# Attention probabilities left unnormalised in a two-block float32 transformer kernel: row sums from the value product, scaling behind it

## What is computed

```python
# GQA: 8 query heads, 2 key/value heads, width 64; MLA: 8 heads, width 96 (keys) and 64 (values)
def blocked_attention(q, k, v, scale):
    ...
    def one_block(qblk):                      # 128 queries
        sc = jnp.einsum('bqhgd,bkhd->bhgqk', qblk, k).astype(jnp.float32) * scale
        p = jax.nn.softmax(sc, axis=-1).astype(v.dtype)
        return jnp.einsum('bhgqk,bkhd->bqhgd', p, v)

# token mixer: ya = GQA attention, yb = MLA attention
merged = g_a * (ya @ w_branch_a) + g_b * (yb @ w_branch_b)
return merged @ w_o
```

## Time and profile before

| | us |
|---|---|
| three runs: median (lowest to highest) | 2943.45 (2938.77 to 2945.5) |
| the profiled execution's own time | 2941.37 |
| its span, first to last instruction | 2939.6 |
| TensorE busy with matmuls | 2820.3 (96%) |
| VectorE, ScalarE, GpSimd busy | 1624.9, 1168.5, 753.2 |

### The profile page before, as it was taken

One profiled execution on the slowest core, in us unless ns is written; L12 is line 12 of the kernel. 1 busy time (PEld: TensorE's weight loads), 2 busy tenths in 40 slices (PEclk: granted clock), 3 DMA queues, 4 the chain that ended last, 5 costly groups with the idle time before them and its releaser, 6 DMA issues.

```text
span 2939.6 us, 34972 instructions
## 1 busy us (share of the span) xinstructions
PE 2820.3 (96%) x13382; PEld 2333.7 (79%) x13382; DVE 1624.9 (55%) x2135; ACT 1168.5 (40%) x1840; POOL 753.2 (26%) x625
## 2 busy tenths in 40 slices
PE   8998999999988999999999888999999999999998
PEld 6676888888876768878888776888887789888887
DVE  5787446334267864464542896555533458565532
ACT  5575334222255753342222554332322338532322
POOL 2464113313125631133131271022200003122210
PEclk9999999999999999999999999999999989999999
DMA  3011222323220112223232211222232210123233
GB/s 138 29 44 37 96 98 80 101 94 100 93 79 29 44 37 95 99 79 108 93 101 93 91 26 61 96 98 96 98 108 93 84 53 1 58 94 97 96 100 101
DMA packets 76279, 236.50 MB, mean 80 GB/s; under 512 B 9904, under 2 KB 19904, under 8 KB 76128
## 3 DMA queue, kind: packets, MB, share of 16 engines
q1 hardware_dynamic: 74928, 231.05, 24.0%
q0 software_dynamic: 928, 3.27, 0.3%
q10 hardware_dynamic: 272, 0.06, 0.0%
HBM read 228.31 MB, written 2.10 MB: 78 GB/s over the span
## 4 chain that ended last, share of the span: by engine, by line
PE 85%; DVE 7%; ACT 3%; issue 2%; SPq 1%; POOL 1%; DMA 1%; POOLq 0%; DVEq 0%; ACTq 0%
PE bank L2063 27%; PE bank L2065 26%; PE bank L2064 26%; PE bank L2472 2%; PE bank L2297 2%; SPq L949 1%; DVE X L1623 1%; DMA RAWW<-weights 1%; DVE STAT L1724 1%; DVE WL L1594 1%; DVE UL L1611 1%; DVE FF L1618 1%; ACT WH L1234 1%; PE bank L2240 0%; DVE FF L1638 0%
## 5 line engine op out<-in xcount | busy, mean ns | idle before, releaser
L1594 DVE TENSOR_TENSOR WL<-RAWW,WH 128x1024 fp32r<-128x1024 f32 (+2 forms) x424 | 573.0, 1355 | 745.2 <-ACT WH L1234 745.0
L2063 PE MATMUL bank<-UH,WH 128*128 128x512 f32 (+2 forms) x1968 | 768.8, 391 | 32.8 <-DVE UL L1611 11.5
L2064 PE MATMUL bank<-UL,WH 128*128 128x512 f32 (+2 forms) x1968 | 760.2, 386 | 0.0
L2065 PE MATMUL bank<-UH,WL 128*128 128x512 f32 (+2 forms) x1968 | 760.2, 386 | 0.0
L1234 ACT ACTIVATE WH<-RAWW 128x1024 fp32r<-128x1024 f32 (+2 forms) x424 | 431.3, 1027 | 401.9 <-DMA RAWW<-weights 401.3
L2063 PEld LDWEIGHTS bank<-UH,WH 128*128 128x128 f32 (+1 forms) x1968 | 372.1, 189 | 119.7 <-issue 22.9
L2064 PEld LDWEIGHTS bank<-UL,WH 128*128 128x128 f32 (+1 forms) x1968 | 372.2, 189 | 75.6 <-issue 2.4
L2065 PEld LDWEIGHTS bank<-UH,WL 128*128 128x128 f32 (+1 forms) x1968 | 371.8, 189 | 75.1
L2063 PE MATMUL bank<-HH,WH 128*128 128x512 f32 (+1 forms) x576 | 210.8, 366 | 0.0
L2065 PE MATMUL bank<-HH,WL 128*128 128x512 f32 (+1 forms) x576 | 210.5, 365 | 0.0
L2064 PE MATMUL bank<-HL,WH 128*128 128x512 f32 (+1 forms) x576 | 210.5, 365 | 0.0
(11 more groups left out here) (366 smaller groups left out, 4783.3 us busy)
## 6 DMA issues: line engine op xcount, KB each, us to landing
RAWW<-weights SPq DMA_DIRECT2D x424, 512.0 KB, 3.4
X<-x SPq DMA_DIRECT2D x8, 256.0 KB, 5.0
FF<-tables POOLq DMA_DIRECT2D x2, 1024.0 KB, 7.9
U<-S5U SPq DMA_DIRECT2D x32, 64.0 KB, 2.0
out<-FF SPq DMA_DIRECT2D x16, 128.0 KB, 1.8
GEL<-U SPq DMA_DIRECT2D x112, 16.0 KB, 1.8
S5B<-s_b POOLq DMA_DIRECT2D x1, 512.0 KB, 4.5
S5C<-s_c POOLq DMA_DIRECT2D x1, 512.0 KB, 3.7
```

What stands on the lines that cost most here:

```text
L1594: dve.tensor_tensor(slot_words(WL, c % SLOTS, size), slot_words(RAWW, c % SLOTS, size), f32(slot_words(WH, c % SLOTS, size)), ALU.subtract ...
L2063: nc.tensor.matmul(out_, w[0], x_[0], start=start, stop=False, **how)
L2064: nc.tensor.matmul(out_, w[0], x_[1], start=False, stop=False, **how)
L2065: return nc.tensor.matmul(out_, w[1], x_[0], start=False, stop=stop, **how)
```

## The change

Seven edits go together.

1. The exponential has no accumulated sum any more, VectorE no reciprocal, GpSimd no multiplication. The tile that is transposed is the exponential itself. `TMP` has three buffers for it and not four; the fourth becomes `Y`.
2. The stationary high part of the values has 64 columns of ones beside the head's 64 value columns (`values_high`), so bank 6 holds the head's unnormalised output on rows 0 to 63 and the row sums, repeated, on rows 64 to 127. The low part has 64 columns alone. The number of matmuls is the same.
3. Behind the values ScalarE takes the logarithm of the sums from the bank and then exp(-log) in place (`att_out_sum`), VectorE multiplies the output by that into `Y` (`att_out_scale`, which frees bank 6), ScalarE copies the high part (`att_out_cut`) and VectorE subtracts (`att_out_low`).
4. Every stage from the transpose on moves one `x` earlier against the scores: transpose at `u + 2`, `att_lo` at `u + 3`, the values from `4h + 7`, `att_out_sum` and `att_out_scale` at `4h + 10`, `att_out_cut` and `att_out_low` at `4h + 11`.
5. GpSimd writes ones (a memset of 128 x 512 at the start of a layer, two of 128 x 256 before the MLA values) in place of zeros (four of 128 x 256).
6. `VL` is made by two VectorE instructions of half the size.
7. To make room, two constant matrices are loaded later with the mask, and the second block's parameters (`SP_`) are loaded by GpSimd's queue in the second layer and not at the very start.

```diff
     for x in range(n + 8):
-        h, phase = divmod(x - KT - 4, KT)
+        h, phase = divmod(x - KT - 3, KT)
+        if 1 <= h <= 2 * HEADS and phase == 0:
+            plan.add("att_out_cut", h=h - 1, pv=h - 1)
         if 0 <= h < 2 * HEADS and phase == 3:
-            plan.add("att_out_hi", h=h, pv=h)
+            plan.add("att_out_sum", h=h, pv=h)
...
-        if 1 <= x <= n:
-            plan.add("att_normalise", u=x - 1)
-        if 3 <= x <= n + 2:
-            plan.add("att_transpose", u=x - 3, h=(x - 3) // KT, t=(x - 3) % KT)
+        if 2 <= x <= n + 1:
+            plan.add("att_transpose", u=x - 2, h=(x - 2) // KT, t=(x - 2) % KT)
...
+        if 1 <= h <= 2 * HEADS and phase == 0:
+            plan.add("att_out_low", h=h - 1, pv=h - 1)
+        if 3 <= x <= n + 2:
+            plan.add("att_lo", u=x - 3, h=(x - 3) // KT, t=(x - 3) % KT)
         if 0 <= h < 2 * HEADS and phase == 3:
-            plan.add("att_out_lo", h=h, pv=h)
+            plan.add("att_out_scale", h=h, pv=h)
...
+        Y = TMP[:, RING, :]
+        def values_high(h, k):
+            if h < HEADS:
+                return VH[:, k, h % 2 * 2:h % 2 * 2 + 2, :].rearrange("p g d -> p (g d)")
+            return MVH[:, h % 2, k, :]
...
-                elif st.kind == "att_normalise":
-                    pool.wait_ge(recip.sem, recip.after(l, st.u))
-                    pool.tensor_tensor(TMP[:, st.u % 4, :], TMP[:, st.u % 4, :],
-                                       STAT[:, 2, st.u % 4:st.u % 4 + 1].to_broadcast([P, SEQ]), ALU.mult
-                                       ).then_inc(normed.sem, 1)
...
-                    act.activation(TMP[:, r, :], BANK[2 + st.u % 2][:], ACT.Exp, bias=STAT[:, 0, r:r + 1],
-                                   accum_out=STAT[:, 1, r:r + 1]).then_inc(expd.sem, 1)
+                    act.activation(TMP[:, st.u % RING, :], BANK[2 + st.u % 2][:], ACT.Exp, bias=STAT[:, 0, r:r + 1]
+                                   ).then_inc(expd.sem, 1)
...
+                elif kind == "att_out_sum":
+                    act.wait_ge(pv.sem, pv.after(l, st.pv))
+                    if st.h:
+                        act.wait_ge(y_l.sem, y_l.after(l, st.pv - 1))
+                    act.activation(Y[0:HD, :], OUTB[HD:P, :], ACT.Ln).then_inc(y_log.sem, 1)
+                    act.wait_ge(y_log.sem, y_log.after(l, st.pv))
+                    act.activation(Y[0:HD, :], Y[0:HD, :], ACT.Exp, scale=-1.0).then_inc(y_factor.sem, 1)
+                elif kind == "att_out_cut":
                     h, _, rows, k = pv_place(st.h)
-                    act.wait_ge(pv.sem, pv.after(l, st.pv))
-                    act.activation(h[rows, k, :], OUTB[rows, :], ACT.Copy).then_inc(y_h.sem, 1)
+                    act.wait_ge(y_scaled.sem, y_scaled.after(l, st.pv))
+                    act.activation(h[rows, k, :], Y[rows, :], ACT.Copy).then_inc(y_h.sem, 1)
...
-                elif kind == "att_normalise":
-                    r = st.u % 4
-                    dve.wait_ge(expd.sem, expd.after(l, st.u))
-                    dve.reciprocal(STAT[:, 2, r:r + 1], STAT[:, 1, r:r + 1]).then_inc(recip.sem, 1)
...
-                elif kind == "att_out_lo":
+                elif kind == "att_out_scale":
+                    _, _, rows, _ = pv_place(st.h)
+                    dve.wait_ge(y_factor.sem, y_factor.after(l, st.pv))
+                    dve.tensor_tensor(Y[rows, :], OUTB[0:HD, :], Y[0:HD, :], ALU.mult).then_inc(y_scaled.sem, 1)
+                elif kind == "att_out_low":
                     h, lo_, rows, k = pv_place(st.h)
                     dve.wait_ge(y_h.sem, y_h.after(l, st.pv))
-                    rest(lo_[rows, k, :], OUTB[rows, :], h[rows, k, :]).then_inc(y_l.sem, 1)
+                    rest(lo_[rows, k, :], Y[rows, :], h[rows, k, :]).then_inc(y_l.sem, 1)
...
                         if st.h:
-                            pe.wait_ge(y_l.sem, y_l.after(l, st.h - 1))
+                            pe.wait_ge(y_scaled.sem, y_scaled.after(l, st.h - 1))
...
                     for k in st.keys:
-                        v = (VH[:, k, :], VL[:, k, :]) if st.h < HEADS else (MVH[:, st.h % 2, k, :], MVL[:, st.h % 2, k, :])
-                        ins = product(OUTB[:], v, (ph[:, k, :], pl[:, k, :]), k == 0, k == KT - 1)
+                        nc.tensor.matmul(OUTB[:], values_high(st.h, k), ph[:, k, :], start=k == 0, stop=False)
+                        nc.tensor.matmul(OUTB[0:HD, :], values_low(st.h, k), ph[:, k, :], start=False, stop=False)
+                        ins = nc.tensor.matmul(OUTB[:], values_high(st.h, k), pl[:, k, :], start=False, stop=k == KT - 1)
```

More of the change, by code:

```diff
@@ L80 @@
 LAST_BANK, FACTOR_BANK = 2, 7
+RING = 3
 LAST_LEAD, POST_MIX, POST_FFN = 2, 4 + QT, 7 + QT
@@ L700, in build @@
         SPARE = at("SPARE", A0 + 16, [P, 2, SEQ])
-        VH = at("VH", A0 + 20, [P, KT, P], F32R)
-        VL = at("VL", A0 + 22, [P, KT, P], F32R)
+        VH = at("VH", A0 + 20, [P, KT, 4, HD], F32R)
+        VL = [at(f"VL{k}", kb, [P, KT // 2, P], F32R) for k, kb in enumerate((204.5, 206))]
         CH = at("CH", A0 + 24, [P, CQT + CKT, SEQ], F32R)
@@ L776, in build @@
         PA = at("PA", 207, [P, 5, PAIRS])
-        MASK = at("MASK", 98, [P, P])
+        MASK = at("MASK", 98, [P, 3, P])
         IDENT, ONES, ONES_HEAD = (MAT[:, k, :] for k in range(3))
-        ROT_A, ROT_B, NEG_TRI, NEG_ONES = (MATR[:, k, :] for k in range(4))
+        ROT_A, ROT_B = (MATR[:, k, :] for k in range(2))
+        NEG_TRI, NEG_ONES = (NEG[:, k, :] for k in range(2))
         BANK = [ctx.enter_context(nc.psum_tensor(f"bank{k}", [P, SEQ], F32)) for k in range(8)]
@@ L806, in build @@
         mats_cut = ctx.enter_context(nc.semaphore("mats_cut"))
-        mv_zero, k_zero = (ctx.enter_context(nc.semaphore(k)) for k in ("mv_zero", "k_zero"))
+        v_ones, mv_ones, k_zero, sp_params = (ctx.enter_context(nc.semaphore(k)) for k in ("v_ones", "mv_ones", "k_zero", "sp_params"))
         x_done = signal("x_done", "x", PN)
@@ L869, in own_square, with pv_place @@
             return {"q": (None, RKV[:], RCQ[:], spare[0]), "cq": (spare[1], RKV[:], RCQ[:]), "ckv": (spare[1], RKV[:])}[st.what][st.i]
+        def pv_place(h):
+            if h < HEADS:
+                a = h % 2 * HD
+                return QH, QL, slice(a, a + HD), h // 2
+            m = h - HEADS
+            return YBH, YBL, slice(m % 2 * HD, m % 2 * HD + HD), m // 2
         def raw(st):
@@ L1020, in step @@
                     pool.tensor_tensor(CL[:, k, :], CF[:, k, :], f32(CH[:, k, :]), ALU.subtract).then_inc(c_l.sem, 1)
[L1021 to L1025 removed]
                 elif st.kind == "evac_br_b":
+                    if l == LAYERS - 1 and st.m == 0:
+                        pool.wait_ge(pv.sem, pv.after(l, HEADS - 1))
+                        pool.dma_start(SP_[:], second_params[:, 0:S_A]).then_inc(sp_params, 16)
                     pool.wait_ge(bank_free.sem, bank_free.after(l, st.j))
@@ L2291, in step @@
                 elif kind == "att_transpose":
-                    pe.wait_ge(normed.sem, normed.after(l, st.u))
+                    pe.wait_ge(expd.sem, expd.after(l, st.u))
                     if st.u == 0:
```

75 lines of the change are left out of this document (37 added, 38 removed).

## The result

| | us |
|---|---|
| changed kernel, median of 13 runs (lowest to highest) | 2949.11 (2947.62 to 2951.42) |
| kernel before, median of 13 runs | 2947.38 (2938.77 to 2950.58) |
| ratio, with its 95% interval | 1.0015 (1.0008 to 1.0022) |
| the profiled execution's own time, and its span | 2949.42, 2947.6 |

The ratio is the record's estimate from all the single runs; the two medians by themselves give 1.0006. Its interval lies above 1, so the changed kernel is a little slower, by less than the 0.2% that the prediction took as the least that can be told apart. The forecast was 2931 us, with 2946 as its upper end. The kernel before ran towards the upper end of its own spread beside it, the execution whose rows are shown ahead (2941.4 us) near the lower.

A forecast was written before the change was run, and what follows sets the result against it. TensorE, busy 96% of the span, was taken as the bound, with gains only from its attention waits and low clock. Terms -9.4 - 7.5 - 1.7 - 1.0 + 0.5 + 5.5 + 3.4 = -10.2 gave 2931 us, range 2919 to 2946.

The forecast's parts named there:

- Bounds: TensorE, busy 96%, bounds; only its attention idling and low clock can change; long transpose waits come from VectorE's `latent` beside GpSimd.
- The four long waits: Transposes in both attentions waiting 13.2 us; `latent` freed from GpSimd, about 1.0 us stays at each; gain 9.4 us.
- The clock behind them: Low-clock stretches of 41 TensorE instructions behind the attentions' long transpose waits vanish; gain 7.5 us.
- Where the change lengthens the path: Bank 6's logarithm, exponential, multiplication: ten uncovered head ends wait 0.6 us each, 6.0 replacing 5.5; loss 0.5 us.
- the 13 small ones: Short transpose waits in both attentions, together 5.5 us, forecast to disappear and be replaced by waits for the multiplication.
- The last MLA head: Wait for its rotated query falls from 2.1 to 1.3 us per layer; gain 1.7 us, plus 1.0 of low clock.
- The ends: Each attention's end: head 15 wait 2.2 us, remade input tile 4.4; loss 5.5 us, plus 3.4 of low clock.
- Loads and parameters, priced at nothing: Later loads of constants and parameters cost nothing, since TensorE waits for none; 0.1 us each if they appeared.
- The slower one: Rival, chance 0.12: bank 6 becomes the bound, its longer chain exposed at all 30 head ends; 2949 us.
- The blocked latents (first rival): Rival, chance 0.14: GpSimd's remaining work still delays `latent`, the long transpose waits stay at 1.6 to 2.9 us; 2941 us.
- a new table load in the attention: Rival, chance 0.01: ScalarE's logarithm might need its own table, charging a load for each change of set.
- What would show it: Signs of being right: `latent` and transpose waits never above 1.5 us, full clock mid-attention, `UL` wait about 4.4 us.

The follow-up runs named there:

- the kernel with the late low part: Changed kernel with VectorE taking the probabilities' low part ahead of the head's own at each head's end; 2942.38 us, ratio 0.9996 to the kernel before.
- the single wait: Changed kernel, head's low part behind the probabilities', late state-space parameters waited for only ahead of the first piece on ScalarE and VectorE; 2945.39 us, ratio 1.0006.
- The changed kernel with the last chain behind the chunks: Changed kernel with only the last head's sum, scaling, cut and low part moved behind the remade input tiles and first two cut weight chunks; 2942.01 us, ratio 0.9987.

## Why the prediction was wrong

**Bounds: right in the main.** GpSimd's normalisation was in the main the cause of the four long waits. Taking it away alone gave 12 us; one latent of each layer stayed at 2.11 us there, and is free (0.75 us) only in the changed order.

**The four long waits: right, slightly undersized.** Forecast 3.8 us left; the four places now wait 1.26, 1.31, 1.25 and 1.30 us, 5.1 in all. `latent` takes 0.73 to 0.75 us but for one in each layer, of 1.50 and 1.54. All four waits are down to 0.15 us in sum once VectorE's two low parts are exchanged. The rule of the Trainium skill that the prediction weighed (SBUF — State Buffer, "Who interferes with whom") also agrees with what stands in the new order: the `MKL` pair, with two SBUF inputs, took 2.39 us beside GpSimd's L1042 and 1.28 in the kernel with the late low part.

**The clock behind them: right.** No low stretch is left behind the four places. In the second profile of the changed kernel there is one of 3.4 us at 957 us, by the 1.9 us wait behind the `MKL` pair, which the sum had not foreseen.

**Where the change lengthens the path: here it failed.** The step was "They take the place of the 13 small ones of 5.5 us, which came from scores, transpose, scores, transpose with no values between, an order that the covered heads no longer have. Loss **0.5**." The multiplication's waits are 4.3 us for the forecast 6.0 (1.01, 0.71 and 0.42 in the first layer). But the transposes' small waits didn't go; they are 20.3 - 5.1 = 15.2 us where they were 5.5. So the term is 19.5 - 5.5 = +14.0, and not +0.5, which takes back most of the 16.9 us of the two terms ahead of it. The other waits came out near their forecasts (-8.1 for -9.4, -1.6 for -1.7, +5.4 for +5.5), the low clock at the ends too (+4.0 for +3.4). From the first scores to the state-space block the marks give +2.6 us where the forecast was -10.2. This one step, 13.5 us off, is about the whole of that miss; the terms as measured add up to +5.2, so waits count for somewhat more here than the time shows.

What the runs show of the cause is the order of VectorE's queue at each head's end. I counted the low part's 0.60 us of work ahead of the probabilities' low part, and not that it waits there for ScalarE's copy, which is itself behind an exponential and other copies. Exchanging the two lines took 8.9 us off the transposes' waits and 6 to 8 us off the time; 5.0 of the 8.9 lie at the four places and 3.9 at the small waits. Of the small waits 11.3 us stay, so the order explains 3.9 of the 9.7 us by which they outgrew 5.5. The rest is not the shift's chain of maximum and exponential, since every transpose that waits starts behind a low part; what holds the low parts up there is open. The removal alone, with the old order and no shift, has 13.7 us of transposes' waits, more than the exchanged order's 11.4. What still separates those two kernels, 11 us (0.9996 against 0.9959), shows mainly at the ends: 9.0 us of waits before value matmuls against 3.0, 8.7 for `UL` against 4.6 with the low clock behind it, and the state-space block, 128.2 us against 124.3.

**The last MLA head: right.** 1.3 us stay in each layer, as forecast.

**The ends: right, to the size of the low clock.** The wait for head 15's values is 2.15 us (forecast 2.2), that for `UL` 4.35 (4.4), and the clock fell behind both, ten instructions each, 2.0 us for 1.7. (The loss of 2.8 us twice is 5.6, where the sum has 5.5.) What I had not looked for was that the placing was free to choose: moved behind weights that were already cut, the chain leaves 1.7 us of each wait and no low clock behind it, and the median is 9.3 us lower, of which the stages place only a part at the ends.

**Loads and parameters, priced at nothing: open.** The state-space block takes 3.4 us longer in the changed kernel. Its marks are GpSimd's memset of S5M and the last start of a matmul on it; first the kernel before:

```profile
L2404 PE MATMUL bank<-U,S5M x128: 275/275/418, 1688.0 to 1749.1; 128*128 128x128 f32 x128
...
L1128 POOL MEMSET S5M<- x1: 6980/6980/6980, 1624.4 to 1624.4; 128x8192 f32 x1
```

Then the changed one:

```profile
L2431 PE MATMUL bank<-U,S5M x128: 275/275/422, 1695.2 to 1757.0; 128*128 128x128 f32 x128
...
L1148 POOL MEMSET S5M<- x1: 6960/6960/6960, 1628.9 to 1628.9; 128x8192 f32 x1
```

That is 124.7 us and 128.1. In the second profiles it is 124.7 and 128.0, so it is no accident of one execution. It is 128.2 in the kernel with the late low part and the single wait, but 124.7 again in the one that differs from it at the ends of the attentions alone, the later of them 540 us earlier; its marks there:

```profile
L2434 PE MATMUL bank<-U,S5M x128: 275/275/422, 1686.1 to 1745.3; 128*128 128x128 f32 x128
...
L1150 POOL MEMSET S5M<- x1: 6982/6982/6982, 1620.6 to 1620.6; 128x8192 f32 x1
```

The changed kernel with the last chain behind the chunks has the later loads and the repeated waits and takes 124.9 us. So neither the later loads nor the repeated waits cost it. All three kernels that move the last head's chain have the short block (124.7 to 124.9); of the seven other executions with the change's loads, six have 127.6 to 128.2 us and one 125.7. The low-clock stretches fall otherwise there; why they do is open.

**The rivals.** The slower one came to 2949 us, the time measured, but that is luck: its mechanism, 30 exposed head ends, didn't happen. TensorE waited for the multiplication six times before the last heads. What happened ran through VectorE's queue to the transposes. The blocked latents (first rival) didn't happen either, nor a new table load in the attention, nor waits of transposes for the exponential (a sign of being wrong that the prediction named), though the view of waits seems to show them. Of "What would show it", two marks stood (4.35 us for `UL`, the clock in the middle in the first profile); L1696 passed its bound of 1.5 by 0.04 at most; and "no L2297 above 1.5 us" was wrong by the 1.85 and 1.86 us behind the `MKL` pair.

## What to carry to other kernels

An instruction with a short duration costs its queue what it waits for, so at each place of an in-order queue ask when its input comes, and put what nobody reads soon behind what TensorE waits for. When a chain is lengthened, look for every place where it stands ahead of something else with a reader, and try it one or two steps later: the stall must have work behind it there, or it only moves on, as it did from `UL` to `WL`. Test a removal by itself before the structure that it needs: here the removal gave 12 us and the structure took them. Where an instruction waits for two things, check which by the handover, 0.15 us here, before believing the name in a view. And split a gain by stages: of 9.3 us in the median, 3.4 lay in a block that the edit does not touch.

## What was not expected of the hardware

Two profiles of one kernel can repeat each other to 0.05 us over an attention (216.02 and 216.00), and those of another differ by 1.35 and 2.7 us (216.29 and 217.64, 214.89 and 217.60). In the changed kernel's second execution a low-clock stretch stands at 268 and one at 957 us that its first lacks. Where low-clock stretches come and go between executions of one program, a term for the clock is worth a range and not a value.

The same instructions of the state-space block took 124.7 us in one kernel and 128.2 in another whose program differs only 540 us and more ahead of them. Both kernels of which there are two profiles repeated their value to 0.1 us. A change of a few us in one stage can so be overlaid by one of 3 us in another that it doesn't touch.
